# First FFN by Strassen's method, and the second layer's modulation in 48 tiles, in a two-layer trunk

## What is computed

```
mod = silu(c) @ ada_w[i] + ada_b[i]           # 6 parts of 1024: shift, scale, gate, twice
h = h + gt_m * mixer(rms_norm(h) * (1 + sc_m) + sh_m)
gate, up = split((rms_norm(h) * (1 + sc_f) + sh_f) @ ffn_w_in[i])     # 1024 -> 2 x 2816
h = h + gt_f * ((silu(gate) * up) @ ffn_w_out[i])                     # 2816 -> 1024
```

## Time and profile before

| what | before |
|---|---|
| median of three executions | 1298.87 us |
| the profiled execution, its time | 1305.82 us |
| its span | 1304.2 us, 19810 instructions |
| TensorE matmul, weight load | 1260.0 us (97%), 1073.5 us (82%) |
| VectorE, ScalarE, GpSimd busy | 864.0, 582.7, 181.0 us |
| moved by DMA | 163.34 MB, mean 125 GB/s |
| mean granted clock of TensorE | 0.986 of full speed |

### The profile page before, as it was taken

How to read it: one execution, slowest core, us unless ns; L and a number is a source line. 1 busy time by engine, 2 the same in 40 slices (tenths; PEclk the granted TensorE clock), 3 DMA queues, 4 the chain that set the end, 5 groups by cost and what they waited for, 6 DMA issues and landing times.

```text
span 1304.2 us, 19810 instructions
## 1 busy us (share of the span) xinstructions
PE 1260.0 (97%) x7915; PEld 1073.5 (82%) x7915; DVE 864.0 (66%) x1045; ACT 582.7 (45%) x747; POOL 181.0 (14%) x242
## 2 busy tenths in 40 slices
PE   5999999899999999999999999999999999999997
PEld 3588788788788888888888888887879989988995
DVE  3799976567876663466467466455789458846865
ACT  6444752444432222222334476556575335523543
POOL 4007964930000000000000000000500000000000
PEclk8999999989999999999999999999999999999999
DMA  9593625425248763377233221112232243325212
GB/s 338 160 145 122 188 76 154 140 86 173 66 122 286 232 222 105 112 241 240 59 90 129 97 65 65 57 57 81 65 97 82 80 126 101 97 75 146 83 59 90
DMA packets 207475, 163.34 MB, mean 125 GB/s; under 512 B 31790, under 2 KB 197899, under 8 KB 205355
## 3 DMA queue, kind: packets, MB, share of 16 engines
q1 hardware_dynamic: 204496, 137.02, 36.3%
q0 software_dynamic: 2400, 25.20, 5.3%
q10 hardware_dynamic: 506, 0.12, 0.0%
HBM read 157.21 MB, written 4.19 MB: 124 GB/s over the span
## 4 chain that ended last, share of the span: by engine, by line
PE 76%; DVE 9%; POOL 5%; ACT 5%; issue 2%; DMA 1%; ACTq 0%; POOLq 0%; DVEq 0%; SPq 0%
PE banks L622 17%; PE banks L624 17%; PE banks L623 17%; PE banks L1365 5%; PE banks L1367 5%; PE banks L1366 5%; DVE wlo L2144 2%; PE banks L937 2%; PE banks L1272 1%; PE banks L927 1%; PE banks L1234 1%; DVE hn_lo L2194 1%; POOL scan_a L3048 1%; DMA raw<-in_ffn_w_in_dram 1%; DVE tmp L2188 1%
## 5 line engine op out<-in xcount | busy, mean ns | idle before, releaser
L2144 DVE TENSOR_TENSOR wlo<-raw,whi 128x2048 fp32r<-128x2048 f32 (+4 forms) x116 | 229.1, 1976 | 87.5 <-ACT whi L1529 41.4
L622 PE MATMUL banks<-hn_hi,whi 128*128 128x512 f32 x688 | 273.8, 398 | 5.2 <-DVE hn_lo L2292 2.2
L624 PE MATMUL banks<-hn_hi,wlo 128*128 128x512 f32 x688 | 270.2, 393 | 0.0
L623 PE MATMUL banks<-hn_lo,whi 128*128 128x512 f32 x688 | 270.2, 393 | 0.0
L622 PE MATMUL banks<-ff_hi,whi 128*128 128x512 f32 x416 | 163.3, 392 | 0.0
L624 PE MATMUL banks<-ff_hi,wlo 128*128 128x512 f32 x416 | 162.0, 389 | 0.0
L623 PE MATMUL banks<-ff_lo,whi 128*128 128x512 f32 x416 | 162.0, 389 | 0.0
L622 PEld LDWEIGHTS banks<-hn_hi,whi 128*128 128x128 f32 x688 | 130.5, 190 | 36.0 <-DVE hn_lo L2194 3.5
L624 PEld LDWEIGHTS banks<-hn_hi,wlo 128*128 128x128 f32 x688 | 130.4, 190 | 27.7
L623 PEld LDWEIGHTS banks<-hn_lo,whi 128*128 128x128 f32 x688 | 130.7, 190 | 26.2
L1535 ACT ACTIVATE whi<-raw 128x2048 fp32r<-128x2048 f32 (+1 forms) x35 | 65.3, 1866 | 148.8 <-PE banks L624 148.8
(11 more groups left out here) (569 smaller groups left out, 2647.0 us busy)
## 6 DMA issues: line engine op xcount, KB each, us to landing
raw<-in_ffn_w_in_dram SPq DMA_DIRECT2D x88, 512.0 KB, 4.9
ada_in<-in_ada_w_dram POOLq DMA_DIRECT2D x16, 1536.0 KB, 6.3
raw<-in_sb_w_in_dram SPq DMA_DIRECT2D x24, 512.0 KB, 4.4
raw<-in_hy_w_in_dram SPq DMA_DIRECT2D x20, 512.0 KB, 5.9
ada_in<-in_ada_w_dram SPq DMA_DIRECT2D x18, 512.0 KB, 4.4
ada_first<-in_ada_w_dram SPq DMA_DIRECT2D x8, 1024.0 KB, 15.0
raw<-in_ffn_w_out_dram SPq DMA_DIRECT2D x32, 256.0 KB, 3.1
raw<-in_ffn_w_out_dram SPq DMA_DIRECT2D x16, 384.0 KB, 4.0
```

The source lines that it names most:

```text
L622: pe.matmul(o, lh, rh, start=first, stop=False)
L623: pe.matmul(o, lh, rl, start=False, stop=False)
L624: return pe.matmul(o, ll, rh, start=False, stop=last)
L2144: TTO(wlo[s][:, 0:width], raw[s][:, 0:width], whi[s][:, 0:width].bitcast(F32), SUB)\
```

## The change

The first FFN gets the program of the second: groups of 6, 8 and 8 tiles, 4 plain slots and 18 Strassen slots, by one `ffn(L)` for both layers. The order of the first sums of the activations changes for both: the fourth sum is written over a part of `hn_hi` and `hn_lo` that is no longer needed, at the first Strassen slot. The second layer's modulation is made in 48 tiles of 128 x 1024, from two buffers: tiles 0 to 4 beside output blocks of the first group, 5 to 12 behind the low sums of the second group's 8 slots, 13 to 18 beside its output blocks, 19 to 23 behind slots of the third group, and 24 to 47 among VectorE's steps of the first two pairs of heads. A fold follows every eighth tile. The gate tiles of the first layer move: four ahead of the factor of the norm, four behind residuals. Six scale tiles of the first layer are loaded behind the S5 results, and the matmuls of their fold stand at head 2 instead of head 0.

```
-HALVES = (12, 10)
-FT = sum(HALVES)
+FT = 22
...
-THIRDS = (8, 8, 6)
+THIRDS = ((6, 8, 8), (8, 8, 6))
...
-            sp.wait_ge(ada_used, 18)
-            for t in range(2, 5):
-                scale_tile(t)
             sp.wait_ge(y_out, 128)
...
-            for t in range(5, 8):
+            sp.wait_ge(ada_used, 18)
+            for t in range(2, 8):
                 scale_tile(t)
...
-                if hd == 0:
+                if hd == 2:
                     pe.wait_ge(block_free, B_GLU + 1)
                     folded_parts(0, 2, 3, 1)
...
+            def ada1_tiles(first, last):
+
+                for u in range(first, last):
+                    t = u % 8
+                    in_, acc = (ada1_in, ada1_acc) if u < 24 else (ada2_in, ada2_acc)
+                    dve.wait_ge(ada1_ld[u % 2], 16 * (u // 2 + 1))
+                    if t == 0:
+                        TS(acc[:, :], in_[u % 2][:, :], c_act[:, t:t + 1], None, MUL).then_inc(ada_used, 1)
+                    else:
+                        dve.wait_ge(ada_used, 32 + u)
+                        STT(acc[:, :], in_[u % 2][:, :], c_act[:, t:t + 1], acc[:, :], MUL, ADD)\
+                            .then_inc(ada_used, 1)
+                    if t == 7:
+                        dve.wait_ge(ada_used, 33 + u)
+                        folded = fold(acc, (0, 1, 0, 0, 1, 2)[u // 8])
...
+            ADA_IN_STAGE = {(0, 0): (0, 1, 2, 3, 4, 5), (0, 1): (13, 15, 16, 17, 18, 19)}
+            ADA_IN_SLOT = {(0, 1): (5, 6, 7, 8, 9, 10, 11, 12, 13), (0, 2): (19, 20, 21, 22, 23, 24, 24, 24, 24)}
...
+                        if not last:
+                            low_sums(q + 1)
+                        if (L, t) in ADA_IN_SLOT:
+                            ada1_tiles(*ADA_IN_SLOT[(L, t)][q - qs[0]:q - qs[0] + 2])
...
+                        if m < 6:
+                            lo(slot + 2 + m, (slot + m) % 2, n_in * P)
+                        if (L, t) in ADA_IN_STAGE and m < 5:
+                            ada1_tiles(*ADA_IN_STAGE[(L, t)][m:m + 2])
...
             for p_ in range(3):
                 a, b = 2 * p_, 2 * p_ + 1
+
+                def late_tiles(first, last):
+                    if p_ < 2:
+                        ada1_tiles(24 + 12 * p_ + first, 24 + 12 * p_ + last)
+
                 magnitudes(a)
+                late_tiles(0, 2)
                 softplus(a)
+                late_tiles(2, 3)
                 softplus_lo(a)
                 magnitudes(b)
                 next_lo(p_ + 1, 0)
+                late_tiles(3, 6)
                 exponents(a)
+                late_tiles(6, 7)
                 softplus(b)
+                late_tiles(7, 8)
                 softplus_lo(b)
                 next_lo(p_ + 1, 1)
+                late_tiles(8, 10)
                 exponents(b)
+                late_tiles(10, 11)
                 out_lo(a)
+                late_tiles(11, 12)
...
+            for u in range(48):
+                part, t = u // 8, u % 8
+                if u == 0:
+                    pool.wait_ge(t_summed, after_one(4))
+                elif u == 24:
+                    pool.wait_ge(block_done, B_SB)
+                if u >= 2:
+                    pool.wait_ge(ada_used, 31 + u)
+                dst = (ada1_in if u < 24 else ada2_in)[u % 2]
+                pool.dma_start(dst[:, :], ada_w[1].rearrange("(p t) n -> p t n", t=8)[:, t, part * D:(part + 1) * D])\
+                    .then_inc(ada1_ld[u % 2], 16)
```

More of the change, by code:

```diff
@@ L1192, in _, with plain_slot @@
-            ffn(0, 16, B_FF0, 1)
+            def plain_slot(L, j, between=None):
+                n = IN_SLOT[L][0] + j
+                slot_ready(n)
+                mh, ml = halves(whi[n % 2]), halves(wlo[n % 2])
+                for two in range(2):
+                    if j == 2:
+                        pe.wait_ge(pair_steps, pair_value(2 * L + 1, 1))
+                    else:
+                        pe.wait_ge(block_free, 2 * n + two - 3)
+                    for k in range(KT):
+                        last = pass3(bank[2 * (j % 2) + two][:, :], mh[:, k, two, :], ml[:, k, two, :],
+                                     hn_hi[:, k, :], hn_lo[:, k, :], k == 0, k == KT - 1)
+                        if between is not None and two == 1 and k == 5:
+                            between()
+                    last.then_inc(block_done, 1)
@@ new lines, in out_block @@
+            def out_block(L, t, m, between=None):
+                n, n_in = OUT_SLOT[L][t] + m, THIRDS[L][t]
+                mh, ml = (x_[n % 2][:, 0:n_in * P].rearrange("p (k m) -> p k m", k=n_in) for x_ in (whi, wlo))
+                slot_ready(n)
+                pe.wait_ge(block_free, 2 * n - 6 if m >= 4 else 2 * OUT_SLOT[L][t] - 2)
+                for k in range(n_in):
+                    if m == 0 and k == n_in - 1:
+                        pe.wait_ge(block_free, 2 * OUT_SLOT[L][t])
+                    last = pass3(bank[m % 4][:, :], mh[:, k, :], ml[:, k, :], ff1_hi[:, k, :], ff1_lo[:, k, :],
+                                 k == 0, k == n_in - 1)
+                    if between is not None and k == 1:
+                        between()
+                last.then_inc(block_done, 2)
@@ L1418, in _ @@
-            first_pair(71, B_FF1, 3, (0, 1), sums_at=2, rows_at=4)
-            as_tiles_come(72, B_FF1 + 2, 3, (2, 3), halves)
-            plain_slot(2)
-            plain_slot(3)
-            for t in range(3):
-                with pe.Fori(0, (LAST_Q[t] + 1 - FIRST_Q[t]) // 2) as i:
-                    for j in range(2):
-                        strassen_slot(Q_SLOT[FIRST_Q[t]], FIRST_Q[t], i, j)
-                for m in range(KT):
-                    out_block(t, m)
-                    if t == 2 and m > 0:
-                        to_tokens(m - 1)
+            ffn(1)
```

1046 lines of the change are left out of this document (446 added, 600 removed).

## The result

The changed kernel takes 1334.67 us (median of four executions, 1327.75 to 1335.9) where the kernel before, run beside it, takes 1299.68 (four, 1298.19 to 1300.91): a ratio of 1.0259, 95% interval 1.0221 to 1.0296. The change costs 35 us. The forecast was 1324.5, range 1306 to 1336, slower with 0.88.

The account below looks back on a forecast made before the run. The kernel was taken as the sum of TensorE's matmul pitches, VectorE nearly full beside Strassen's sums. -14.2 + 10.9 + 1.2 + 5.7 + 16.9 + 5.1 = +25.6 us, added to the 1298.9 median, gave 1324.5 us, range 1306 to 1336.

Parts of the forecast that it names:

- no rival: Rivals: 1314.4 us (chance 0.2), 1313.6 (0.1), 1304 (0.05), 1290.4 (0.08), 1299 (0.02).
- Saving, -14.2: First FFN: 18 slots at 10.05 us as Strassen instead of 10.85 plain, 0.79 saved each, all on the path.
- the spacing rule of the Trainium skill: TensorE matmul spacings of 131 ns at 512 columns, some 98 at 256: 18 slots would lose 35 us; left out of the sum.
- Slots, +10.9: First FFN's Strassen slots: a tile stalls TensorE 0.7 us, 12 times, and two folds add 1.25 each; bounds +6 and +13.
- the ring: Strassen slots: third product, its copy, sum_hi, ff_hi, ff_lo form a closed chain, so each tile slot pays the stall again.
- Start, +1.2: First FFN's start: the gate tiles' fold moves ahead of the input sums, where VectorE has no idle time; 0 to 2 us.
- Boundaries, +5.7: First FFN's group boundaries: next weights come late, 4.6 us behind the group of 6, 1.05 at the other; bounds +3 and +8.
- Attention, +16.9: First two head pairs: 1.7 us before first heads' sums, 10.2 before second heads', 4.95 load waits; bounds +11 and +19.
- Own work of VectorE: Attention: five tiles and a fold between the two low parts stall TensorE 5.1 us in each of the first two pairs.
- Waits for loads: Attention: with two buffers VectorE waits for the third tile in a row, 3.1 us in the first pair, 1.85 in the second.
- The first head's slack: Attention: 0.13 us before the first head's sums, so one tile ahead of its low parts stalls TensorE 0.85 us, twice.
- Clock, +5.1: Three new long stalls, one per pair and one at the first boundary, drop TensorE to 1.2 GHz, 1.7 us each; 0 to 10.

Follow-up runs that it names:

- no_tiles: Changed kernel without the second layer's 48 modulation tiles, their loads and folds (zeros instead), leaving only Strassen's method in the first FFN; 1295.25 us, ratio 0.9946.
- loads_held: Changed kernel with the loads of tiles 6 and 20 held back on POOL until the next group's first weights have landed; 1330.09 us, ratio 1.0224.
- groups_886: Changed kernel with the first FFN's groups in the order 8, 8, 6 instead of 6, 8, 8; 1326.49 us, ratio 1.0203.
- late_no_loads: Changed kernel with all 24 attention tiles computed but only the first two loaded, the two buffers being read again; 1325.44 us, ratio 1.019.
- late_in_waits: Changed kernel with the attention's 24 tiles spread over places where VectorE waits, same two buffers and loads; 1323.9 us, ratio 1.0174.
- all_moved: Changed kernel with slot tiles before VectorE's wait, attention tiles in idle time, groups 8, 8, 6 and two tile loads held; 1309.13 us, ratio 1.0071.
- early_undone: Changed kernel with the first layer's scale tile loads and the place of their fold's matmuls put back as before; 1334.3 us, ratio 1.0256.
- no_late_tiles: Changed kernel without the attention's 24 modulation tiles, their loads and three folds, zeros in place of their results; 1310.31 us, ratio 1.0069.

## Why the prediction was right, and where it was off

**Direction, places and mechanism held; the size is in part luck.** Every stall stands where the prediction put it, with the releaser it named (later_lo, sq, wlo), and no rival describes the run. The change costs 35.0 us where the sum said 25.6. The 1334.67 lies 1.3 us under the upper end of the range, and it does so because the slots cost 3 us less than forecast, while the boundaries (10.6, bounds 3 to 8) and the clock (10 to 11, bounds 0 to 10) reached or passed their own upper bounds. By its steps:

- **Saving, -14.2:** 14.1 to 14.3 by no_tiles. Of the spacing rule of the Trainium skill (TensorE: Matmul & The Clock Gate, Back-to-back issue gap), by which the change would lose 35 us here, the runs show nothing. (The estimate of 98 ns for 256 columns lies a third of the way between the two spacings, as the columns do, and not halfway.)
- **Slots, +10.9:** 7.9 measured. The size was right (0.63 for 0.7, 2.04 for 0.7 + 1.25), the count not: eight slots pay, not twelve. The slot behind a group's first tile doesn't, in either group (the ring isn't closed yet); nor the one behind tile 8, which is a plain product of 0.75 us; nor the last of the middle group, where no sums for a next slot stand between tile and gate sum.
- **Start, +1.2:** 0.6.
- **Boundaries, +5.7:** 10.6 measured in the profiled execution, 7.5 to 12.0 in the five others with the same program here. no_tiles gives 5.5, nearly the step's own number, so the short cover of a group of 6 was right. The tiles bring the rest, 4.9 us in the profiled execution; the step had their loads in its bound only. loads_held shows that most of the second boundary's excess goes with the load held; groups_886 shows that the load alone doesn't make it.
- **Attention, +16.9:** 18.7. Own work of VectorE 5.1 a pair forecast, 5.07 and 4.33 by late_no_loads. Waits for loads 3.1 and 1.85 forecast, 4.65 and 3.65 read as waits on VectorE, 4.5 and 3.5 by late_no_loads: the 3.7 us from issue to landing was an interpolation between sizes, and this load, issued 1.3 us behind the weights' 1024 KB, took 5.7 (770.53 to 776.27). The first head's slack was right (0.61 for 0.85).
- **Clock, +5.1:** 10 to 11. It was costed at 1.7 a stall from one stretch of 3.3 us; the stretches at the three long stalls are 6.8 and twice 10.2 us long, partly idle, and hold 4.4 to 5.7 us of work each, and two of 3.4 us that I hadn't counted follow (477.7, 576.7). This is the term that was mis-sized most.
- **The base.** The sum was read from a profiled execution 7 us above its median and added to the median. That was right: the excess is the two half-clock stretches of that execution, which the profiled one of the changed kernel lacks, and no part of the change.

Terms off by -3.0, -0.6, +4.9, +1.8 and +6.0 make +9.1, and 25.6 + 9.1 = 34.7 is the measured 35.0 within what executions differ (8 us between the fastest and the slowest of the changed kernel's four).

**What stays open.** The half-clock stretches near 262 and 940 us come and go between runs whose program is the same there; no run tells what decides it. What delays the weights at the boundaries in the order 6, 8, 8 and not in 8, 8, 6, with the same tile load beside them, is open too. The third buffer and the places of the threes weren't tried apart. And neither less work for VectorE nor an earlier load of the weights was tried at the attention's entry.

## What to carry over

Strassen's method paid its arithmetic, about 14 us. What came with it cost over three times that, and nearly all of it came back by other places for the tiles, a third load buffer and another order of the groups. A filler of 1.3 us belongs behind the last low part that TensorE waits for, or where the engine already waits, never ahead of such a low part when it has no slack, and averages of busy time don't tell the two apart. Count a filler's loads like its work. With two buffers the third tile of a row waited 4.65 and 3.65 us for its load; with as many buffers as tiles in a row none waited. And a filler's load beside the load that ends a wait is a risk: it cost up to 3.7 us here, or nothing.

## What the runs showed that I had not expected

- 24 loads of 512 KB in the attention cost nothing with three buffers, in threes (window at 178 GB/s instead of 69, TensorE 46.00 of 46.00), while late_in_waits and all_moved, with two and the tiles spread over other places of idle time, kept about 10 us of stalls there.
- The order of the groups (6, 8, 8 or 8, 8, 6) doesn't remove the stall behind the short group; it moves it to the next stage (5.74 at the first boundary became 1.03 there and 4.43 at the attention's entry). The second boundary's fall from 4.88 to 0.66 came with it, for no reason that the group's length gives.
- The stall at one boundary differs by up to 2.5 us between executions with the same program there (2.37 to 4.88 us at the second), by how long the weights take to land (7.0 to 9.5 us from the issue of their second half).
- A stall's price at a fallen clock is not a constant: the granted 0.50 held for 10.2 us after gaps of 9.6 and 7.9 us, for 6.8 us around one of 5.7 and for 3.4 us behind one of 4.9. Behind shorter gaps it could go either way: it fell after one of 2.37 (early_undone) and not after one of 2.94 (no_late_tiles).
